# Doubling levels of a triangular inverse on every second block of columns, in a two-layer encoder kernel

## The chip, the cores and the metric

The kernel runs on one NeuronCore of a Trainium2 chip. TensorE does matrix products out of SBUF into PSUM, VectorE, ScalarE and GpSimd work elementwise, SyncE starts most transfers. The metric is the device time of one execution in microseconds, lower is better. All data are fp32. A profile records each instruction of one execution and the clock that TensorE was granted.

## What is computed

Two layers of a bidirectional encoder on 256 tokens of width 1024. Each layer has a SwiGLU block, a mixer of three branches and another SwiGLU block. The change touches the first branch, RWKV-7 time mixing with 16 heads of 64, forwards and backwards:

```python
def rwkv7_scan(r, w, k, v, a, b, reverse):
    """Generalised delta rule: S_t = S_{t-1} diag(w_t) + (S_{t-1} a_t) b_t^T + v_t k_t^T, y_t = S_t r_t."""
    ...
    def step(state, inp):
        r_t, w_t, k_t, v_t, a_t, b_t = inp
        sa = jnp.einsum("bhij,bhj->bhi", state, a_t)
        state = (state * w_t[:, :, None, :] + sa[..., None] * b_t[:, :, None, :]
                 + v_t[..., None] * k_t[:, :, None, :])
        return state, jnp.einsum("bhij,bhj->bhi", state, r_t)
```

The kernel doesn't run this token by token. It cuts the 256 tokens into 4 chunks of 64. Within a chunk the dependence of each token on the earlier ones is a triangular 64x64 matrix, and what is needed is the inverse of (identity minus that matrix), for each head, chunk and direction.

## The kernel before

**Data.** Heads are handled in pairs, 8 pairs a layer. A tile has 128 partitions: 64 for the first head of the pair, 64 for the second. The helper by_head issues one matmul for each head, 64 contraction rows and 64 weight columns each, so that the two use different quarters of the array. Each fp32 matmul appears in a trace as two weight loads and two matmul records. All matmuls have the line of the helper mm (L787), all two-tensor VectorE operations L1478 or L1484.

**One pair** (pair_body) goes in this order. First come products of the scaled keys with the stacked operands (64x192 and 64x64 forms), for each direction d, with masks on VectorE; they give the triangular matrix mb[:, d, c, 0:L] and the first inverse of 2x2 blocks, dd[:, d, 0] (called D), and its transpose dd[:, d, 1]. Pairs 1 to 3 also carry two products of the conditioning vector with 512-column weights (late_modulation), one before each half. Then comes the doubling stage, then the recurrence over the four chunks, into which the preparation of the next pair is woven (pair_lora, pair_bonus).

**The doubling stage** has LV = 5 levels. At level k the diagonal blocks of width h = 2 << k are already inverted, and the level joins two neighbours. For each direction d TensorE forms F = mb times D into PSUM bank 2 + d (8 matmuls, 64 moving columns each). VectorE multiplies F by the mask lvl[:, d, k + 1], which keeps only the blocks that join two neighbours, and writes E into ee[:, d]. TensorE forms D times E and E times the transposed D into bank 4 + d (16 matmuls for each direction; the last level forms only the second, 8). VectorE adds both onto dd[:, d] in one operation. Four semaphores hold the order: f_done, e_ready, de_done, dd_ready. TensorE's queue is F for d = 0, F for d = 1, DE for 0, DE for 1; VectorE's is mask 0, mask 1, addition 0, addition 1. VectorE waits for each of its own operations before the next one (raised). Nothing else is queued on either engine within the stage.

**Buffers.** All stage tensors are cut from one scratch tile by a carver. ee is [2, CH, L], and two buffers of the group norm, yy and ysq, lie in it. On GpSimd's queue, at the beginning of the branch, stand two loads of weights, two copies of an identity into the operand tile ar (signal eyes_ready), and then the four weight loads of pair 0 (pair_loads); everything later on that queue waits for the pairs.

Of the kernel before, what the change touches and what calls it, by code (L numbers as in the profile page):

```python
# [15 lines left out]
ALU = mybir.AluOpType  # L16
# [4 lines left out]
P = 128  # L21
# [94 lines left out]
def build(nc, a, out):  # L116
    with ExitStack() as ctx:
# [92 lines left out]
        dd = carve([2, 2, CH, L])  # L210
        ee = carve([2, CH, L])

        yy, ysq = ee[:, 0], ee[:, 1]
        rs = carve([2, L])
# [205 lines left out]
        def settle(eng):  # L420

            eng.sem_inc(settled, 1)

        block = ctx.enter_context(nc.Block())
# [109 lines left out]
        def _(pool):  # L534
# [70 lines left out]
            for l in range(DEPTH):  # L605
# [46 lines left out]
                for d in range(2):  # L652
                    ins = pool.tensor_copy(ar[:, d, :, 2, :], eye)
                    if d == 0:
                        own.step(ins)
                ins.then_inc(eyes_ready.sem, 1)
                pool.wait_ge(*eyes_ready(l, 1))
# [127 lines left out]
        def _(pe):  # L785
# [89 lines left out]
            for l in range(DEPTH):  # L875
# [104 lines left out]
                def pair_body(p, first, last, late=None):  # L980
# [29 lines left out]
                    for k in range(LV):  # L1010
                        w = p * 2 * LV + 2 * k
                        for d in range(2):
# [6 lines left out]
                            for c in range(CH):  # L1019
                                ins = by_head(ps[:, 2 + d, c * L:(c + 1) * L], mb[:, d, c, 0:L], dd[:, d, 0, c, :])  # L1020
                            ins.then_inc(f_done.sem, 1)
                        for d in range(2):
                            pe.wait_ge(*e_ready(l, w + d + 1))
                            for c in range(CH):
                                if k < LV - 1:
                                    by_head(ps[:, 4 + d, c * L:(c + 1) * L], dd[:, d, 1, c, :], ee[:, d, c, :])
                                ins = by_head(ps[:, 4 + d, S + c * L:S + (c + 1) * L], ee[:, d, c, :], dd[:, d, 1, c, :])
                            ins.then_inc(de_done.sem, 1)
# [445 lines left out]
        def _(dve):  # L1474
# [69 lines left out]
            for l in range(DEPTH):  # L1544
# [197 lines left out]
                def pair_body(p, first, last, late=None):  # L1742
# [37 lines left out]
                    for k in range(LV):  # L1780
                        w = p * 2 * LV + 2 * k
                        for d in range(2):
                            dve.wait_ge(*f_done(l, w + d + 1))
                            raised(tt(ee[:, d], ps[:, 2 + d, 0:S].rearrange("p (c t) -> p c t", c=CH),
                                      lvl[:, d, k + 1:k + 2, :].to_broadcast(b4), ALU.mult), e_ready(l, w + d + 1))
                        for d in range(2):
                            dve.wait_ge(*de_done(l, w + d + 1))
                            u0 = 0 if k < LV - 1 else 1
                            both = dd[:, d, u0:2].rearrange("p u c t -> p (u c t)")
                            raised(tt(both, both, ps[:, 4 + d, u0 * S:2 * S], ALU.add), dd_ready(l, w + d + 1))  # L1790

# [338 lines left out]
```

## Time and profile before

| | |
|---|---|
| median of 3 runs | 4291.69 us (4289.75 to 4297.94) |
| the profiled execution: its own time | 4294.79 us |
| its span, first to last instruction | 4293.1 us |
| mean granted clock of TensorE | 0.85 of full speed (1.00 is 2.4 GHz, 0.50 is 1.2 GHz) |
| busy: TensorE, weight loads, VectorE | 3354.0, 2316.1, 1398.4 us |
| the doubling stages | 16, at about 555 to 1013 us and 2690 to 3152 us |

A line of the page's groups gives line, engine, operation, the tiles written and read, their shapes, the count and the mean time. Idle time in front of a group counts only where nothing else was running that the end waits for. A busy TensorE is not one at its peak: the time of a record includes its way through the array, and records overlap; their pace shows in how many fit into a stretch.

### The profile page before, as it was taken

To read this page: it belongs to the slowest core of one execution; us is meant where nothing else is said; L and a number is where in the kernel's file an instruction comes from. 1 tells how busy PE (TensorE), PEld (TensorE's weight loads), DVE (VectorE), ACT (ScalarE), POOL (GpSimd) and SP (SyncE) were. 2 spreads that over 40 slices of the span, in tenths; PEclk is the share of its full clock that TensorE was granted. 3 is DMA by queue.
4 is the path that set the end of the run, shared out by engine and by line. 5 is a ranking of instruction groups with operands and counts; after the bars stand their busy time and mean duration, and the time that the engine had idled before them with its cause. 6 is when DMAs were issued, how large, how long until landed. Compare 5 with 4: busy or idle time off the path is not lost.

```text
span 4293.1 us, 50048 instructions
## 1 busy us (share of the span) xinstructions
PE 3354.0 (78%) x22117; PEld 2316.1 (54%) x22117; DVE 1398.4 (33%) x2502; ACT 373.8 (9%) x764; POOL 209.6 (5%) x352
## 2 busy tenths in 40 slices
PE   6998778778855588679969986887787655887798
PEld 4666565565443436447646665655554533364476
DVE  1002555662136601410010025555522266024100
ACT  0000201010111000200000011001001110001000
POOL 4000000000001100000000000000000011000000
PEclk9999888778975599789989988897898755997899
DMA  6553212001311123034445522120023120331343
GB/s 212 176 181 107 96 48 67 23 4 60 134 65 60 39 99 137 20 122 151 148 163 183 189 102 90 48 82 6 4 69 131 59 68 31 119 118 40 118 147 108
DMA packets 234938, 410.51 MB, mean 96 GB/s; under 512 B 6601, under 2 KB 101383, under 8 KB 234721
## 3 DMA queue, kind: packets, MB, share of 16 engines
q1 hardware_dynamic: 224672, 378.81, 25.6%
q0 software_dynamic: 10048, 28.49, 2.2%
q8 instruction: 174, 2.85, 0.3%
q14 instruction: 44, 0.35, 0.0%
HBM read 406.10 MB, written 1.18 MB: 95 GB/s over the span
## 4 chain that ended last, share of the span: by engine, by line
PE 65%; DVE 18%; issue 8%; DMA 4%; ACT 3%; POOL 1%; DVEq 0%; SPq 0%; POOLq 0%; ACTq 0%
PE ps L787 63%; DVE scratch L1478 7%; DVE scratch L1484 4%; DVE scratch L1481 3%; DMA ring<-in_ffn_w 1%; DMA scratch<-acs_scratch 1%; DMA ring<-in_w_in 1%; ACT scratch L1396 1%; DVE merged L1652 1%; DVE hT L1481 1%; ACT scratch L1263 0%; DMA scratch<-in_norm_w 0%; DVE scratch L1666 0%; PE ps L1132 0%; PE ps L819 0%
## 5 line engine op out<-in xcount | busy, mean ns | idle before, releaser
L787 PE MATMUL ps<-scratch 64*64 64x64 f32 (+5 forms) x14112 | 1201.7, 284 | 373.9 <-DVE scratch L1478 126.2
L787 PEld LDWEIGHTS ps<-scratch 64*64 64x64 f32 (+2 forms) x14112 | 840.0, 160 | 717.3 <-issue 203.3
L787 PE MATMUL ps<-hT,ring 128*128 128x256 f32 (+1 forms) x4992 | 1125.4, 388 | 59.6 <-DVE hT L1481 29.2
L787 PEld LDWEIGHTS ps<-hT,ring 128*128 128x128 f32 (+1 forms) x4992 | 971.0, 195 | 223.8 <-DVE hT L1481 31.4
L1478 DVE TENSOR_TENSOR scratch<-scratch,ps 128x512 f32<-128x512 f32 (+3 forms) x312 | 202.0, 647 | 1303.9 <-ACT scratch L1273 781.2
L787 PE MATMUL ps<-ring,hT 128*128 128x512 f32 x896 | 411.9, 622 | 29.9 <-DMA ring<-in_w_in 16.0
L1478 DVE TENSOR_TENSOR scratch<-scratch 128x512 f32<-128x512 f32 (+5 forms) x452 | 302.8, 670 | 61.1 <-DMA scratch<-acs_scratch 21.6
L787 PEld LDWEIGHTS ps<-ring,hT 128*128 128x128 f32 x896 | 177.9, 200 | 257.6 <-issue 223.5
L787 PE MATMUL ps<-ring,ccol 128*128 128x512 f32 x576 | 262.4, 613 | 2.4 <-DMA ring<-in_ada_w 2.4
L787 PE MATMUL ps<-ring,scratch 128*128 128x512 f32 x512 | 221.7, 592 | 0.0
L787 PEld LDWEIGHTS ps<-ring,ccol 128*128 128x128 f32 x576 | 113.4, 199 | 143.3 <-issue 137.3
L1484 DVE SCALAR_TENSOR_TENSOR scratch<-ps,prm,scratch 128x254 f32<-128x254 f32 x192 | 92.6, 482 | 234.7 <-ACTq L1399 228.3
L787 PEld LDWEIGHTS ps<-ring,scratch 128*128 128x128 f32 x512 | 97.3, 190 | 122.5 <-issue 122.5
L1132 PE MATMUL ps<-ident,scratch 128*128 128x128 f32 x80 | 19.7, 427 | 134.9 <-DVE scratch L1478 134.9
L1273 ACT ACTIVATE scratch<-ps 128x512 f32<-128x512 f32 x44 | 26.3, 597 | 1110.9 <-PE ps L787 1110.9
L1478 DVE TENSOR_TENSOR scratch<-ps,lvl 128x256 f32<-128x256 f32 x224 | 95.1, 425 | 81.9 <-PE ps L787 76.8
L1484 DVE SCALAR_TENSOR_TENSOR scratch<-ps,der,scratch 128x255 f32<-128x255 f32 (+1 forms) x112 | 54.0, 482 | 151.3 <-ACTq L1300 147.8
L1481 DVE TENSOR_SCALAR scratch<-scratch 128x64 f32<-128x64 f32 (+6 forms) x256 | 86.5, 338 | 42.8 <-ACTq L1453 19.9
L1132 PEld LDWEIGHTS ps<-ident,scratch 128*128 128x128 f32 x80 | 15.7, 223 | 139.0 <-DVE scratch L1478 139.0
L603 POOL TENSOR_TENSOR stat<-stat,mhalf 128x2 f32<-128x2 f32 x12 | 8.5, 704 | 1382.6 <-DVE stat L1481 1382.6
L819 PE MATMUL ps<-ident,scratch 128*128 128x128 f32 x96 | 21.9, 421 | 67.9 <-DVE scratch L1481 67.9
L1478 DVE TENSOR_TENSOR prow<-ps,ident 128x512 f32<-128x512 f32 x24 | 16.6, 692 | 149.4 <-PE ps L787 149.4
(206 smaller groups left out, 1339.7 us busy)
## 6 DMA issues: line engine op xcount, KB each, us to landing
ring<-in_w_in SPq DMA_DIRECT2D x56, 2048.0 KB, 7.8
ring<-in_ffn_w SPq DMA_DIRECT2D x88, 1024.0 KB, 7.9
ring<-in_ada_w SPq DMA_DIRECT2D x36, 2048.0 KB, 7.9
scratch<-in_ffn_w SPq DMA_DIRECT2D x44, 1024.0 KB, 5.1
ring<-in_w_branch_mamba SPq DMA_DIRECT2D x8, 2048.0 KB, 8.0
scratch<-acs_scratch POOLq DMA_DIRECT2D x32, 512.0 KB, 5.2
ring<-in_w_branch_rwkv SPq DMA_DIRECT2D x4, 2048.0 KB, 8.5
ring<-in_w_branch_diff SPq DMA_DIRECT2D x4, 2048.0 KB, 7.9
```

Source lines behind the costliest of these rows:

```text
L603: pool.tensor_tensor(stat[:, 4:4 + n], stat[:, 2:2 + n], mhalf[:, 0:n], ALU.pow).then_inc(rstd_ready.sem, 1)
L787: return pe.matmul(o, lhsT, rhs, start=start, stop=stop)
L819: ins = pe.transpose(o, xn[:, t, kt * P:(kt + 1) * P], ident[:, :])
L1132: ins = pe.transpose(ps[:, 4 + t, m * P:(m + 1) * P], cv[:, parity, m, t * P:(t + 1) * P], ident[:, :])
L1273: act.activation(sgm[:, j % 2, :], ps[:, 2 * (g % 2), :], ACT.Sigmoid).then_inc(ffn_sig.sem, 1)
L1396: own.step(act.activation(cv[:, parity, m, :], ps[:, 2 * ((g + parity) % 2) + m // 2, (m % 2) * S:(m % 2 + 1) * S], ACT.Identity, scale=pr ...
L1478: return dve.tensor_tensor(o, i0, i1, op)
L1481: return dve.tensor_scalar(o, i0, s1, s2, op0, op1)
L1484: return dve.scalar_tensor_tensor(out=o, in0=i0, scalar=s, in1=i1, op0=op0, op1=op1)
L1652: own.step(dve.reciprocal(kk_sq_buf, kk_sq_buf))
```

## The change

At each level only every second block of the columns can change: for direction 0 the even blocks of D and the odd ones of its transpose, for direction 1 the other way round. The new kernel computes, masks and adds these columns alone. The moving operand of each matmul of the stage is a view of every second block (32 columns in runs of h), its result is packed in PSUM (32 columns for each chunk). The mask reads and writes only the half blocks, and the addition reads 128 packed columns for each of the two products and adds them onto the half blocks of dd. E remains a full 64-column weight operand, whose other blocks have to be zero. So ee becomes five buffers, one for each level, cleared once per layer by GpSimd, and yy and ysq get a space of their own. The numbers of matmuls, weight loads, VectorE operations and semaphore steps stay; one memset per layer is added.

```diff
--- before.py
+++ after.py
@@ -208,9 +208,9 @@
         mb = carve([2, CH, 2 * L])
         mk = carve([2, CH, 2 * L])
         dd = carve([2, 2, CH, L])
-        ee = carve([2, CH, L])
-
-        yy, ysq = ee[:, 0], ee[:, 1]
+        ee = carve([LV, 2, CH, L])
+        yy = carve([CH, L])
+        ysq = carve([CH, L])
         rs = carve([2, L])
         yn = carve([CH, L])
         gstat = carve([4, CH])
@@ -421,6 +421,31 @@
 
             eng.sem_inc(settled, 1)
 
+        def half_blocks(m, k, side):
+
+            return m.rearrange("p (b u i) -> p b u i", u=2, i=2 << k)[:, :, side, :]
+
+        def half_chunks(m, k, side):
+
+            return m.rearrange("p c (b u i) -> p c b u i", u=2, i=2 << k)[:, :, :, side, :]
+
+        def joined(m, k):
+
+            return m.rearrange("p (b i) -> p b i", i=2 << k)
+
+        def half_pair(d, k, us):
+
+            h = 2 << k
+            flat = dd.rearrange("p d u c t -> p (d u c t)")
+            at = d * 2 * S
+            if us == 1:
+                m = flat[:, at + S + (1 - d) * h:at + S + (1 - d) * h + S - h].rearrange("p (a n i) -> p a n i", a=1, i=h)
+            elif d == 0:
+                m = flat[:, at:at + 2 * (S + h)].rearrange("p (a n i) -> p a n i", a=2, i=h)
+            else:
+                m = flat[:, at + h:at + h + 2 * (S - h)].rearrange("p (a n i) -> p a n i", a=2, i=h)
+            return m[:, :, 0:2 * (S // (2 * h)) - 1:2, :]
+
         block = ctx.enter_context(nc.Block())
 
         def halves(pair):
@@ -653,7 +678,8 @@
                     ins = pool.tensor_copy(ar[:, d, :, 2, :], eye)
                     if d == 0:
                         own.step(ins)
-                ins.then_inc(eyes_ready.sem, 1)
+                own.step(ins)
+                pool.memset(ee, 0.0).then_inc(eyes_ready.sem, 1)
                 pool.wait_ge(*eyes_ready(l, 1))
                 own.restart()
                 def pair_loads(q):
@@ -1017,14 +1043,17 @@
                             else:
                                 pe.wait_ge(*btm_evac(l, 2 * p + 2))
                             for c in range(CH):
-                                ins = by_head(ps[:, 2 + d, c * L:(c + 1) * L], mb[:, d, c, 0:L], dd[:, d, 0, c, :])
+                                ins = by_head(joined(ps[:, 2 + d, c * 32:(c + 1) * 32], k), mb[:, d, c, 0:L],
+                                              half_blocks(dd[:, d, 0, c, :], k, d))
                             ins.then_inc(f_done.sem, 1)
                         for d in range(2):
                             pe.wait_ge(*e_ready(l, w + d + 1))
                             for c in range(CH):
                                 if k < LV - 1:
-                                    by_head(ps[:, 4 + d, c * L:(c + 1) * L], dd[:, d, 1, c, :], ee[:, d, c, :])
-                                ins = by_head(ps[:, 4 + d, S + c * L:S + (c + 1) * L], ee[:, d, c, :], dd[:, d, 1, c, :])
+                                    by_head(joined(ps[:, 4 + d, c * 32:(c + 1) * 32], k), dd[:, d, 1, c, :],
+                                            half_blocks(ee[:, k, d, c, :], k, d))
+                                ins = by_head(joined(ps[:, 4 + d, P + c * 32:P + (c + 1) * 32], k), ee[:, k, d, c, :],
+                                              half_blocks(dd[:, d, 1, c, :], k, 1 - d))
                             ins.then_inc(de_done.sem, 1)
                     pe.wait_ge(*dd_ready(l, (p + 1) * 2 * LV))
 
@@ -1781,13 +1810,16 @@
                         w = p * 2 * LV + 2 * k
                         for d in range(2):
                             dve.wait_ge(*f_done(l, w + d + 1))
-                            raised(tt(ee[:, d], ps[:, 2 + d, 0:S].rearrange("p (c t) -> p c t", c=CH),
-                                      lvl[:, d, k + 1:k + 2, :].to_broadcast(b4), ALU.mult), e_ready(l, w + d + 1))
+                            h = 2 << k
+                            found = ps[:, 2 + d, 0:P].rearrange("p (c b i) -> p c b i", c=CH, i=h)
+                            keep = half_chunks(lvl[:, d, k + 1:k + 2, :], k, d).to_broadcast([P, CH, L // (2 * h), h])
+                            raised(tt(half_chunks(ee[:, k, d], k, d), found, keep, ALU.mult), e_ready(l, w + d + 1))
                         for d in range(2):
                             dve.wait_ge(*de_done(l, w + d + 1))
                             u0 = 0 if k < LV - 1 else 1
-                            both = dd[:, d, u0:2].rearrange("p u c t -> p (u c t)")
-                            raised(tt(both, both, ps[:, 4 + d, u0 * S:2 * S], ALU.add), dd_ready(l, w + d + 1))
+                            both = half_pair(d, k, 2 - u0)
+                            gain = ps[:, 4 + d, u0 * P:2 * P].rearrange("p (u n i) -> p u n i", u=2 - u0, i=2 << k)
+                            raised(tt(both, both, gain, ALU.add), dd_ready(l, w + d + 1))
 
                     for j in range(CH):
                         dve.wait_ge(*r_done(l, 4 * p + j + 1))
```

## Rows read from the trace of the kernel before

**Rows 1.** The page: busy time by engine, granted clock by slice, the chain's engines.
```profile
PE 3354.0 (78%) x22117; PEld 2316.1 (54%) x22117; DVE 1398.4 (33%) x2502; ACT 373.8 (9%) x764; POOL 209.6 (5%) x352
...
PEclk9999888778975599789989988897898755997899
...
PE 65%; DVE 18%; issue 8%; DMA 4%; ACT 3%; POOL 1%; DVEq 0%; SPq 0%; POOLq 0%; ACTq 0%
```
**Rows 2.** VectorE's groups by form: names, shapes, count | busy us, mean ns, idle before.
```profile
L1478 DVE TENSOR_TENSOR scratch<-scratch,ps 128x512 f32<-128x512 f32 x232 | 159.7, 688 | 889.3 <-ACT scratch L1273 781.2 <-PE ps L787 105.8
...
L1478 DVE TENSOR_TENSOR scratch<-ps,lvl 128x256 f32<-128x256 f32 x224 | 95.1, 425 | 81.9 <-PE ps L787 76.8
...
L1794 DVE COPY scratch<-ps 128x128 f32<-128x128 f32 x64 | 18.7, 292 | 59.3 <-PE ps L787 59.3
```
**Rows 3.** The chain of waits, pair 2 of layer 0: start us, us, what.
```profile
688.29 0.70 DVE scratch L1478
...
689.03 2.57 PE ps L787 x80
...
691.70 0.70 DVE scratch L1478
...
699.48 0.70 PE ps L787 x16
...
700.27 0.44 DVE scratch L1478
...
700.75 0.70 PE ps L787 x16
...
701.55 0.43 DVE scratch L1478
```
**Rows 4.** Windows, 64 columns on 128: busy of PE, PEld, DVE, ACT, POOL (count), clock, DMA.
```profile
3621.30:3634.80 13.50, 13.50 (x64) 13.50 (x64) 7.21 (x9) 0.00 (x0) 0.00 (x0) 0.50 0.00 0
1298.90:1302.30 3.40, 3.40 (x33) 3.40 (x31) 0.71 (x2) 2.26 (x4) 0.00 (x0) 1.00 0.56 177
```
**Rows 5.** Timeline of TensorE, 64 columns on 64: start us, us, what [idle before].
```profile
588.02 0.69 PE L787 MATMUL ps<-scratch 64*64 64x64 f32 x8 [0.46 <-DVE scratch L1801]
...
713.01 2.44 PE L787 MATMUL ps<-scratch 64*64 64x64 f32 x40 [0.23 <-DVE scratch L1794]
```
**Rows 6.** Windows of six stretches: as in rows 4.
```profile
555.60:570.00 14.40, 13.39 (x410) 12.59 (x412) 9.29 (x17) 0.00 (x0) 0.00 (x0) 1.00 0.01 3
588.10:593.40 5.30, 5.30 (x30) 3.43 (x31) 4.70 (x12) 0.00 (x0) 1.04 (x1) 0.51 0.00 0
593.60:599.00 5.40, 5.40 (x15) 2.23 (x15) 1.84 (x3) 0.00 (x0) 0.00 (x0) 1.00 0.00 0
683.80:686.00 2.20, 1.14 (x33) 1.00 (x32) 1.93 (x4) 0.00 (x0) 0.00 (x0) 1.00 0.41 66
713.00:715.40 2.40, 2.38 (x40) 2.25 (x40) 1.82 (x5) 1.34 (x3) 0.00 (x0) 0.50 0.04 10
789.60:794.60 5.00, 5.00 (x42) 3.88 (x44) 0.34 (x1) 0.00 (x0) 0.00 (x0) 0.50 0.00 0
```
**Rows 7.** The chain of waits, three doubling stages: pauses of TensorE.
```profile
626.47 0.88 issue
...
2767.07 0.71 issue
...
2894.72 0.97 issue
```
**Rows 8.** Timeline of GpSimd at the beginning of the branch, layer 0.
```profile
388.66 0.87 POOL L653 COPY scratch<-stack_i 128x256 f32<-128x256 f32 x2
...
390.25 0.59 POOL L662 DMA_DIRECT2D scratch<-in_rwkv_w  x1 [0.71 <-POOL scratch L653]
...
522.27 0.57 POOL L662 DMA_DIRECT2D scratch<-in_rwkv_w  x1 [129.85 <-PE ps L787]
```
**Rows 9.** The instructions on one tile: GpSimd's largest memset, min/median/max ns.
```profile
L596 POOL MEMSET vfirst<- x1: 1805/1805/1805, 96.5 to 96.5; 128x2048 f32 x1
```

## Prediction

> **What bounds the kernel now.** I read the page first: TensorE is busy 78% of the span and carries 65% of the chain that ended last, VectorE 18% [rows 1]. The granted clock is not uniform: several slices stand at 5 to 8 tenths [rows 1]. Then I read the forms by line to get prices, then the chain of waits inside one doubling stage. There are 16 such stages (8 head pairs, 2 layers), all alike in form. In one steady level the chain is: the second addition of the level before (0.70 us), 0.04 us until TensorE starts, 80 matmul records (2.57 us), 0.10 us until VectorE starts the next addition (691.70 - 689.03 - 2.57) [rows 3]. A record is half a matmul: each fp32 matmul shows as two. The period is 691.70 to 688.29 = 3.41 us. TensorE has 96 records per level; 16 of them (the first half of F) run under the addition, the other 80 (second half of F, 32 of DE for each direction) stand on the path, and the masks lie beside them. The last level has no D half and is a ladder: 16 records 0.70, mask 0.44, 16 records 0.70, addition 0.43 [rows 3]. No DMA, ScalarE or GpSimd step stands in this stage. What ends a level is therefore the pace of the records plus one addition.
>
> **The masks.** 128x256 becomes 128x128. Prices: 425 ns now; 292 ns for 128x128 out of PSUM (a copy, the nearest row) [rows 2]. 133 ns less. On the path this counts only for the mask of the first level (it waits for F and DE waits for it) and for the second mask of the last level: 2 x 0.13 = 0.26 us per stage.
>
> **The additions.** In levels 0 to 3, 128x512 becomes 128x256: 688 to 425 ns (the price of the 128x256 masks, one PSUM and one SBUF operand as well) [rows 2], four on the path: 4 x 0.26 = 1.05 us. In the last level 128x256 becomes 128x128: 0.13 us. The first half of F then starts earlier too, but still ends before the second half may start. The new patterns have runs of 2, 4, 8, 16 and 32 floats, and no VectorE row shows a run shorter than 64. Bounds: no extra cost, or each element of the two shortest runs costs double, which puts masks and additions of those two levels back at the old prices (0.13 + 2 x 0.26 = 0.66 us per stage back). I take no extra cost, since runs of 64 with gaps (the initial masks, in the same group of 224) cost the same 425 ns as dense ones [rows 2]. Below nothing it can't go: the element count is what falls.
>
> **The matmuls.** The moving columns fall from 64 to 32; the number of matmuls, of weight loads and the 64 weight columns stay. Does the pace follow? The trace has a case with few moving columns for its weights: 64 moving columns on 128 weight columns. At full clock 31 weight loads take 3.40 us, 110 ns each, and at the lower clock 64 take 13.50 us, 211 ns [rows 4]; there are eight such stretches, all at 0.50, of which the last is shown. With the same 64 moving columns on 64 weight columns, two heads side by side, one record follows another every (2.57 - 0.70)/64 = 29.2 ns at full clock [rows 3], 58 ns per head, and every (2.44 - 0.69)/32 = 54.7 ns at the lower clock [rows 5, 6]. The same moving columns, half the weight columns, half the time: in these cases the pace follows the weights. So the change leaves 29.2 ns per record. Only the tail of the last record of each block gets shorter; its size isn't shown, I take 0.03 us (6 blocks on the path: about 0.16 us), bounds 0 and 0.05. The other bound for the pace is half of 29.2 ns (rival 2).
>
> The Trainium skill (TensorE: Matmul & The Clock Gate, Back-to-back issue gap) has another floor to the same effect: matmuls of 1 to 64 columns all take about 60 cycles. By that sentence as well the sum keeps its matmul term.
>
> **Sum with the clock as it was:** 0.26 + 1.05 + 0.13 + 0.16 = 1.6 us per stage, 16 stages, 25.6 us. Against the profiled execution (4294.8 us; span 4293.1) that is 4269.2, and 3.1 less for the median of the runs shown (4291.7): 4266.
>
> **The clock.** The stages now run at 1.00 (2.4 GHz) once entered: 555.6 to 570 us at 1.00 [rows 6]. What the engine does before the clock rises or stays is what the change alters. Two stretches in which the records call TensorE busy without a gap go different ways: from 588.1 to 593.4 (64 on 64 columns, then 128 on 256 and 512) the clock is 0.51 and then 1.00 [rows 6]; in all eight stretches of 64 moving on 128 weight columns, 13.5 us each, it stays at 0.50 to the end [rows 4]. There the array streams columns only half of the time that weights are loaded. After the change, the doubling stage has just that ratio: 32 moving on 64 weight columns. So I expect: a stage that is at the lower clock can't climb out of it before its last level is over; and a stage entered at the full clock is much nearer to losing it at every gap than now. The gaps are there: between F and DE of the first level in pairs 1 and 2 VectorE reduces a row first (TensorE busy 1.14 of 2.20 us) [rows 6], and three stages of 16 hold a pause of 0.71 to 0.97 us that the chain calls issue [rows 7]. Today these gaps go by at full clock.
>
> Price of a fall: at 54.7 ns a level is 96 x 54.7 = 5.25 us (TensorE alone, the additions hidden under F) against 3.41, +1.84 per level; in the ladder 32 + 16 records more slowly and two smaller VectorE steps, about +0.6 against now; the start of the recurrence behind it, some 80 records at +25 ns until the clock is back, +2.0. A fall at the pause in the second level costs 2.5 x 1.84 + 0.6 + 2.0 = 7.2 us, one in the first level 4 x 1.84 + 0.6 + 2.0 + 0.8 (rest of its DE) = 10.8 us.
>
> I take five stages: the three with a pause (7.2 each = 21.6), and two more of those with the long gap after F or entered just as the clock rises (10.8 each = 21.6). Eleven stages gain 1.6 = 17.6. Net +25.6: 4294.8 + 25.6 - 3.1 = **4317 us**. What no row says is how near to falling a steady level is. A second unknown: in pairs 4 to 7 the products ahead of each stage start at 0.50 [rows 6], and a rise that doesn't come earlier when they do would eat up to 8 x 1.6 = 13 us of the gain.
>
> **The buffers.** One factor buffer per level instead of one: DE reads all 64 weight columns of it, so the half that isn't written must be zero. GpSimd clears 128x2560 per layer: its 128x2048 clear took 1.81 us [rows 9], so 2.26 us, behind the two copies at 388.66 and ahead of the four loads of pair 0, the first of which starts at 390.25. Those loads then start 2.3 us later; the next command of that queue waits until 522.27 for TensorE [rows 8], so the cover is 130 us. Behind it in GpSimd's queue are only these loads; who waits for them is the first pair's projection, long after. Cost nothing; 2 x 2.3 us without the cover. The moved group-norm buffers add no wait, as VectorE writes them in order.
>
> A rule that speaks against the change would be one on short strides. The Trainium skill (Advanced Engine Details and Errata, Memory Cachelines) asks for at least two hits in a 16-byte line; two floats of every four give exactly two. By it no read slows; if the matmul's read did slow at runs of 2, there is room: its columns now take about half of each record's slot. No row here shows such a read.
>
> **Rivals.**
> 1. The full clock holds, or falls in a stage or two only. For it: today even the pauses pass at 1.00, the steady level keeps 96 records in a shorter period. Against: the eight stretches. Time 4266 with none, up to 4280 with one or two. Chance 0.21. It is on the other side (faster).
> 2. The pace follows the moving columns after all: 80 records at 14.6 instead of 29.2 ns take 1.2 us less per level, some 5 us per stage; 4266 - 80 = 4186. Against it rows 4. Chance 0.04.
> 3. The two cancel: two or three stages fall (some 20 to 30 us back against 21 to 24 gained), or the gain of pairs 4 to 7 is lost ahead of the next stage: 4283 to 4300. Chance 0.15. Short runs that cost VectorE double belong here: 16 x 0.66 = 10.6 us back, 4277, and with one fall 4287.
> 4. A steady level too is beyond what holds the full clock: 13 or more of the 16 fall in their first level: 13 x 10.8 - 3 x 1.6 = +136, 4428. Chance 0.10. It decides from the first level on; the sign is that of the forecast.
> The forecast (3 to 8 stages fall, net gain of time lost 10 to 70 us): 0.50.
>
> **How the numbers follow.** The likeliest case gives 4317; its own range is 4301 to 4362. The range reaches down to 4264 for rival 1 and up to 4352, leaving out rival 2, rival 4 and the top of the forecast case, about 2 in 10. About 0.2% (8.6 us) is what a measurement of this kernel can tell from no change. Faster: 0.21 + 0.04 = 0.25. Same: 0.15. Slower: 0.50 + 0.10 = 0.60.
>
> **What would show it.** VectorE masks at 292 and additions at 425 ns show the first terms; a record pace of 29 ns with 32 columns the third; a steady level of 3.1 us at clock 1.00 the sum. Level stages with a granted clock of 0.50 and levels of 5.2 us show the fall, with the stages of 626 us and 2767 us first. I am wrong if all 16 stages stand at 1.00, if the records come closer than 29 ns, or if steady levels fall without a gap.

## The result, and the profile after

Four runs of the changed kernel have a median of 4349.9 us (4339.3 to 4353.5), four of the kernel before beside them 4293.0 us (4289.8 to 4297.9). The ratio is 1.0127, interval 1.0107 to 1.0148: slower by 57 us at the medians. The profiled execution took 4339.3 us, its span is 44.4 us longer than before. The forecast was slower by 26.

Two words are used throughout: a matmul or a stage is narrow when its records move 32 columns and wide when they move 64; a stage holds when its granted clock stays at 1.00 and falls when it drops to 0.50 (1.2 GHz) within it.

The page of the kernel after: span; busy time by engine; granted clock of TensorE in 40 slices; the chain's engines. They answer to [rows 1].

```profile
span 4337.5 us, 50050 instructions
...
PE 3424.2 (79%) x22117; PEld 2401.4 (55%) x22117; DVE 1338.5 (31%) x2502; ACT 373.6 (9%) x764; POOL 214.0 (5%) x354
...
PEclk9999777777985589699989987787779755897899
...
PE 67%; DVE 16%; issue 8%; DMA 4%; ACT 3%; POOL 1%; DVEq 0%; SPq 0%; POOLq 0%; ACTq 0%
```

VectorE has 60 us less work, as meant. TensorE is busy 70 us longer with the same number of matmuls, and slices 6 to 10 (where the doubling stages of layer 0 lie) read 77777 where they read 88778, and slices 26 to 30 (layer 1) read 78777 where they read 89789. VectorE's forms, line 1507 (the helper for two tensors), the same columns as [rows 2]:

```profile
L1507 DVE TENSOR_TENSOR scratch<-scratch,ps 128x256 f32<-128x256 f32 x128 | 54.0, 422 | 120.9 <-PE ps L813 120.9
...
L1507 DVE TENSOR_TENSOR scratch<-ps,lvl 128x128 f32<-128x128 f32 x160 | 46.7, 292 | 54.0 <-PE ps L813 52.0
```

Masks take 292 ns and the additions of the first four levels 422 ns in the mean over runs of 2 to 32 floats, no more than the prices of dense rows (292 and 425 ns): here short runs cost nothing on VectorE. The chain of waits in pair 6 of layer 0, a stage that keeps the full clock (start us, us, what), answers to [rows 3]:

```profile
943.69 2.54 PE ps L813 x80
...
946.33 0.43 DVE scratch L1507
...
946.80 2.55 PE ps L813 x80
...
949.44 0.43 DVE scratch L1507
...
958.04 0.30 DVE scratch L1507
```

The period is 949.44 - 946.33 = 3.11 us where it was 3.41. The 80 records still take 2.55 us: halving the columns left the pace alone. In this stage the change does what it was costed at. Now the stages by windows: 14.5 us from the first mask of twelve of the 16 (the eight of layer 0, then pairs 1, 2, 3 and 7 of layer 1). Columns: window, length, busy of PE, PEld, DVE, ACT, POOL (count), clock, DMA.

```profile
552.40:566.90 14.50, 13.73 (x432) 13.06 (x432) 6.71 (x20) 0.00 (x0) 0.00 (x0) 1.00 0.02 5
616.20:630.70 14.50, 14.13 (x278) 14.13 (x280) 4.28 (x12) 0.00 (x0) 0.00 (x0) 0.54 0.38 143
689.30:703.80 14.50, 14.04 (x300) 13.93 (x300) 4.81 (x14) 0.00 (x0) 0.00 (x0) 0.61 0.38 141
759.00:773.50 14.50, 13.63 (x424) 12.84 (x420) 6.71 (x20) 0.00 (x0) 0.00 (x0) 1.00 0.44 149
813.90:828.40 14.50, 14.50 (x298) 14.45 (x296) 4.48 (x13) 0.00 (x0) 0.00 (x0) 0.55 0.01 2
878.90:893.40 14.50, 14.50 (x295) 14.45 (x294) 4.38 (x13) 0.00 (x0) 0.00 (x0) 0.55 0.01 2
943.80:958.30 14.50, 13.61 (x431) 12.90 (x428) 6.84 (x20) 0.00 (x0) 0.00 (x0) 1.00 0.02 5
1001.70:1016.20 14.50, 14.50 (x296) 14.50 (x298) 4.38 (x13) 0.00 (x0) 0.00 (x0) 0.55 0.01 2
2780.20:2794.70 14.50, 14.11 (x278) 14.11 (x280) 4.29 (x13) 0.00 (x0) 0.00 (x0) 0.54 0.39 142
2852.70:2867.20 14.50, 13.44 (x374) 13.00 (x376) 5.67 (x16) 0.00 (x0) 0.00 (x0) 0.87 0.38 143
2919.90:2934.40 14.50, 12.77 (x316) 12.29 (x314) 4.86 (x14) 0.00 (x0) 0.00 (x0) 0.79 0.44 149
3155.50:3170.00 14.50, 14.50 (x296) 14.45 (x294) 4.38 (x13) 0.00 (x0) 0.00 (x0) 0.55 0.01 2
```

Read the count beside the clock. A stage at 1.00 gets through all 432 records in 14.5 us; one at 0.55 gets through some 296 and is not done for another 8 us, while TensorE shows busy without a gap. Nine stages lose the clock: pairs 1, 2, 4, 5, 7 of layer 0, and pairs 1, 2, 3, 7 of layer 1. Before, all 16 stood at 1.00. The fall within pair 4, and the stretches behind a stage that held (pair 6) and one that fell (pair 4):

```profile
813.90:815.30 1.40, 1.40 (x52) 1.35 (x48) 0.58 (x2) 0.00 (x0) 0.00 (x0) 1.00 0.00 0
815.30:818.00 2.70, 2.70 (x60) 2.70 (x56) 0.88 (x3) 0.00 (x0) 0.00 (x0) 0.52 0.02 6
818.00:828.00 10.00, 10.00 (x192) 10.00 (x192) 2.82 (x8) 0.00 (x0) 0.00 (x0) 0.50 0.01 2
...
958.30:962.30 4.00, 3.92 (x80) 3.92 (x80) 1.18 (x5) 0.00 (x0) 0.00 (x0) 0.57 0.01 4
958.30:1001.70 43.40, 29.82 (x386) 23.64 (x386) 24.04 (x54) 5.79 (x14) 1.01 (x1) 0.65 0.01 1
836.10:878.90 42.80, 28.68 (x390) 22.55 (x392) 24.08 (x54) 5.79 (x14) 3.20 (x5) 0.68 0.03 6
```

The clock falls 1.4 us into the stage and stays at its lower level (1.2 GHz) until the stage is over. And the stage that held loses it just behind its end: the first 4 us of the recurrence behind pair 6 run at 0.57. The same stretches in the kernel before:

```profile
939.30:943.30 4.00, 4.00 (x89) 3.31 (x89) 1.15 (x4) 0.00 (x0) 0.00 (x0) 1.00 0.01 4
939.30:981.20 41.90, 28.36 (x384) 22.00 (x386) 24.02 (x54) 5.79 (x14) 1.01 (x1) 0.67 0.00 1
```

The 43.4 us from the end of a held stage to the next were 41.9. With the stage itself that is 57.9 us, where it was 58.1 (16.2 + 41.9): the 1.6 us that a held stage gains are not kept here.

**The sums.** From the first mask to the last addition of each stage, the 16 stages took 262.4 us before and 296.4 after (+34.0). The 14 stretches between two stages of a layer took 621.3 and 636.8 (+15.6). The rest (start, between the layers, end) is 5.2 less, for which I have no reason. Together +44.4, the difference of the spans. Stage by stage there is one trace, and it is of the fastest of the four runs; its mean clock is 0.825, that of the others 0.822 to 0.824.

### The profile page after: what moved, and what is told of

The parts are those of the page before. It is cut to its first block, busy times and chain, and to the rows that moved or that the text cites. A ratio compares the mean times of both kernels' runs of the same rounds, so it can differ in the third digit from the quotient of the medians.

```text
span 4337.5 us, 50050 instructions
## 1 busy us (share of the span) xinstructions
PE 3424.2 (79%) x22117; PEld 2401.4 (55%) x22117; DVE 1338.5 (31%) x2502; ACT 373.6 (9%) x764; POOL 214.0 (5%) x354
## 4 chain that ended last, share of the span: by engine, by line
PE 67%; DVE 16%; issue 8%; DMA 4%; ACT 3%; POOL 1%; DVEq 0%; SPq 0%; POOLq 0%; ACTq 0%
PE ps L813 65%; DVE scratch L1507 6%; DVE scratch L1513 4%; DVE scratch L1510 3%; DMA ring<-in_ffn_w 1%; DMA scratch<-acs_scratch 1%; DMA ring<-in_w_in 1%; ACT scratch L1425 1%; DVE merged L1681 1%; DVE hT L1510 1%; ACT scratch L1292 0%; DVE scratch L1695 0%; PE ps L1161 0%; DMA scratch<-in_norm_w 0%; PE ps L845 0%
## 5 line engine op out<-in xcount | busy, mean ns | idle before, releaser
L813 PE MATMUL ps<-scratch 64*64 64x32 f32 (+6 forms) x14112 | 1278.0, 306 | 350.9 <-DVE scratch L1507 105.8
L813 PEld LDWEIGHTS ps<-scratch 64*64 64x64 f32 (+2 forms) x14112 | 928.4, 185 | 681.4 <-issue 204.6
L1507 DVE TENSOR_TENSOR scratch<-scratch,ps 128x256 f32<-128x256 f32 (+3 forms) x312 | 163.5, 524 | 1376.0 <-ACT scratch L1302 780.3
L813 PE MATMUL ps<-ring,hT 128*128 128x512 f32 x896 | 410.7, 620 | 30.1 <-DMA ring<-in_w_in 16.2
L1507 DVE TENSOR_TENSOR scratch<-ps,lvl 128x128 f32<-128x128 f32 (+1 forms) x224 | 73.9, 330 | 102.6 <-PE ps L813 99.1
L1510 DVE TENSOR_SCALAR scratch<-scratch 128x64 f32<-128x64 f32 (+6 forms) x256 | 86.3, 337 | 42.8 <-ACTq L1482 19.9
```

What stands on the lines that cost most here:

```text
L813: return pe.matmul(o, lhsT, rhs, start=start, stop=stop)
L1507: return dve.tensor_tensor(o, i0, i1, op)
L1510: return dve.tensor_scalar(o, i0, s1, s2, op0, op1)
```

## The experiments

The theory (A): it is the records with 32 moving columns on 64 weight columns that bring the clock down, and a stage made of them is near its edge. The rivals: the longer chain or the buffers; only the entry or the pauses; the gapped reads. This table has all runs; "fell" counts stages with a clock under 1.00 in the profiled execution, the last two columns are the sums just explained. The median of the kernel before lies between 4290.7 and 4296.7 us in the sets that the variants ran beside, so that the ratios compare better than the medians.

| kernel | median us | ratio to before | fell | 16 stages | 14 between |
|---|---|---|---|---|---|
| before | 4293.0 | 1 | 0 | 262.4 | 621.3 |
| after | 4349.9 | 1.0127 (1.0107 to 1.0148) | 9 | 296.4 | 636.8 |
| wide_pe | 4262.7 | 0.9926 (0.9909 to 0.9942) | 0 | 240.8 | 616.1 |
| de_wide | 4264.3 | 0.9931 (0.9916 to 0.9946) | 1 | 242.4 | 614.3 |
| f_wide | 4270.7 | 0.9945 (0.9928 to 0.9962) | 3 | 249.3 | 617.7 |
| buffers_only | 4297.2 | 1.0009 (1.0000 to 1.0018) | 0 | 261.9 | 621.6 |
| first_level_wide | 4303.1 | 1.0033 (1.0020 to 1.0046) | 4 | 255.1 | 638.9 |
| last_level_wide | 4312.6 | 1.0035 (1.0019 to 1.0050) | 10 | 306.3 | 620.2 |
| ends_wide | 4278.0 | 0.9961 (0.9946 to 0.9976) | 5 | 258.7 | 615.0 |
| slow_add_narrow | 4407.0 | 1.0270 (1.0255 to 1.0285) | 16 | 360.9 | 637.0 |
| slow_add_wide | 4292.1 | 1.0002 (0.9993 to 1.0012) | 0 | 264.4 | 619.8 |
| dense_reads | 4352.2 | 1.0135 (1.0114 to 1.0156) | 10 | 301.0 | 642.8 |
| late_spread_narrow | 4339.9 | 1.0109 (1.0094 to 1.0124) | 10 | 293.9 | 635.9 |
| late_spread_wide | 4255.5 | 0.9917 (0.9902 to 0.9931) | 0 | 243.3 | 606.8 |

**All matmuls wide again (wide_pe).** TensorE computes all 64 columns into full blocks; VectorE still masks and adds only its half, in place.

```diff
-ins = by_head(joined(ps[:, 2 + d, c * 32:(c + 1) * 32], k), mb[:, d, c, 0:L],
-              half_blocks(dd[:, d, 0, c, :], k, d))
+ins = by_head(ps[:, 2 + d, c * L:(c + 1) * L], mb[:, d, c, 0:L], dd[:, d, 0, c, :])
```

> The matmuls of the doubling stage are back to 64 moving columns (F, and both products of DE), written unpacked as before; VectorE's masks and additions stay on half the columns and read them out of PSUM in place. Nothing of the result is left out. Theory A (the clock falls because the matmuls stream half as many columns for the same weight loads): all 16 doubling stages at a granted clock of 1.00, a steady level of 3.12 to 3.15 us, a stage near 14.6 us against 16.15 before; time 4263 to 4275. Theory B (the clock falls because of VectorE's side: shorter steps, strided patterns, or the new buffers): 6 or more stages fall to 0.50 again, 4325 to 4355.

Measured 4262.7 us. Two of its stages (pairs 4 and 6 of layer 0) and the stretch behind pair 6:

```profile
802.90:817.40 14.50, 13.77 (x430) 12.87 (x426) 6.69 (x20) 0.00 (x0) 0.00 (x0) 1.00 0.01 3
...
912.20:926.70 14.50, 13.73 (x430) 12.83 (x425) 6.69 (x20) 0.00 (x0) 0.00 (x0) 1.00 0.02 5
...
926.90:930.90 4.00, 4.00 (x89) 3.31 (x89) 1.15 (x4) 0.00 (x0) 0.00 (x0) 1.00 0.01 4
926.90:966.70 39.80, 24.92 (x386) 19.52 (x388) 24.00 (x54) 5.79 (x14) 1.01 (x1) 0.83 0.01 1
```

The same number of matmuls and weight loads as after, the same VectorE sizes. What differs is the moving columns per record, and with them two patterns: TensorE reads without gaps (dense_reads tries that alone), and its results lie in PSUM unpacked (that alone was not tried). No stage falls, and 87 us are gone. The narrow columns themselves gave 0.16 us a stage (14.68 us here, 14.52 in a held stage after); the other 1.47 us are VectorE's half-size steps.

**One kind of matmul wide (de_wide, f_wide).** de_wide: D and E with 64 columns (64 of the 96 records of a level), F with 32. f_wide the other way.

```diff
-by_head(joined(ps[:, 4 + d, c * 32:(c + 1) * 32], k), dd[:, d, 1, c, :], half_blocks(ee[:, k, d, c, :], k, d))
+by_head(ps[:, 4 + d, c * L:(c + 1) * L], dd[:, d, 1, c, :], ee[:, k, d, c, :])
```

> The changed kernel with DE alone (64 of a level's 96 records) back to 64 moving columns; F stays at 32, VectorE at half. Nothing is left out. Theory A: no stage or one falls, 4263 to 4280, at or below the kernel with wide F. Theory B: 7 to 10 fall, 4325 to 4355.

> The changed kernel with F alone (32 of a level's 96 matmul records) back to 64 moving columns; DE stays at 32, VectorE at half. Nothing is left out. Theory A: fewer stages fall than the 9 of the changed kernel, 1 to 4 of 16, first those with a pause of TensorE or the long gap in the first level; 4270 to 4305. Theory B (not the matmul columns): as many as before, 7 to 10, 4325 to 4355.

With two thirds of the records wide one stage falls (pair 3 of layer 1, after a pause of TensorE of 1.2 us), and only for 3.4 us:

```profile
2878.20:2881.60 3.40, 3.40 (x72) 3.40 (x70) 0.71 (x2) 0.00 (x0) 0.00 (x0) 0.51 0.02 5
2881.60:2887.50 5.90, 5.29 (x160) 4.82 (x156) 3.00 (x9) 0.00 (x0) 0.00 (x0) 1.00 0.01 3
```

With one third wide, three fall, each about 8 us into the stage, in the third level, behind a pause (pair 1 of both layers, pair 3 of layer 1). With 0, 32, 64 and 96 narrow records in a level 0, 1, 3 and 9 stages fall, and neither kind alone gives the nine; whether the share or the kind decides between 1 and 3 isn't told apart.

**The buffers alone (buffers_only).** The kernel before, with a factor buffer for each level, GpSimd's clear and the moved group-norm buffers.

```diff
-ee = carve([2, CH, L])
+ee = carve([LV, 2, CH, L])
+pool.memset(ee, 0.0).then_inc(eyes_ready.sem, 1)
```

> The kernel before with only the buffers of the change: one factor buffer for each level, cleared by GpSimd, and own buffers for the group norm. All operations keep 64 columns. Theory A: 4288 to 4298, stages at 1.00 and 16.15 us, the clear of about 2.3 us under the projection. Rival (the moved buffers or the clear in GpSimd's queue cost): 4300 or more, with the first stage later.

Ratio 1.0009, interval 1.0000 to 1.0018, so that a cost of up to 8 us isn't excluded by the times; the stages (261.9 us) and stretches (621.6 us) are as before, and nothing of the 57 us lies in them. The clear in the kernel after, in GpSimd's timeline:

```profile
386.59 2.23 POOL L682 MEMSET scratch<- 128x2560 f32 x1
...
389.53 0.59 POOL L688 DMA_DIRECT2D scratch<-in_rwkv_w  x1 [0.71 <-remote]
```

It takes 2.23 us (the step said 2.26).

**Only the first level wide, only the last, both.** Levels two to four stay narrow in all three.

```diff
-ins = by_head(joined(...), mb[:, d, c, 0:L], half_blocks(...))
+if k in WIDE:                      # {0}, {4}, {0, 4}
+    ins = by_head(ps[:, 2 + d, c * L:(c + 1) * L], mb[:, d, c, 0:L], dd[:, d, 0, c, :])
+else:
+    ins = by_head(joined(...), mb[:, d, c, 0:L], half_blocks(...))
```

> The changed kernel, but the first of the five doubling levels computes all 64 columns again (matmuls into full blocks, VectorE still masks and adds only its half, in place); levels two to five stay at 32 columns. Theory A (a level whose records carry 32 columns on 64 weight columns gives the clock too little to go by wherever it stands, so that entry decides only part of it): the first level no longer loses the clock, some stages fall later, in levels two or three, at a lower price each (about 4 us instead of 6 to 8); 4285 to 4320 us, with 4 to 9 of 16 stages showing a level at 0.50. Rival B (only the entry decides: the lower half rate of the products ahead, the gap between F and DE of the first level, and the first level itself): once the first level is wide, no stage falls but perhaps the three with a pause, and the time is that of the all-wide variant within a few us, 4260 to 4272.

> Only the last of the five levels computes all 64 columns, levels one to four stay at 32. Theory A: the falls inside the stages stay as in the changed kernel (7 to 10 of 16, in the first or second level); what goes is the late start of the recurrence behind the stages that hold, up to 3.5 us each for about seven stages: 4320 to 4340. Rival C: as the changed kernel, 4345 to 4355.

> First and last of the five levels compute all 64 columns, levels two to four stay at 32. In the traces so far, a narrow stage that held the full clock loses it behind its last level, whose matmuls alternate with VectorE steps: the first 4 us of the recurrence stand at 0.57, and the stretch from stage to stage is 43.4 us, against 39.9 behind a wide stage. Theory A (each narrow stretch brings the clock down behind it, the last level as well): with a wide last level the stretches behind pairs 4 to 7 are 39.8 to 40.1 us, 8 x 3.5 = 28 us less than the first_level_wide variant's 4303: 4270 to 4283, while the falls in levels three and four of the stages with a pause stay (3 to 5 stages). Rival C (the stretch behind the stage depends on when in the recurrence the clock changes, not on the last level): 43 us stays, 4298 to 4306.

first_level_wide: 4303.1 us, inside theory A's numbers, but for half another reason. Four stages fall (pairs 1 and 2 of layer 0, 1 and 3 of layer 1, all in the third or fourth level). Not one of pairs 4 to 7 falls, which rival B had said; where there is neither pause nor long gap, the first level decides in this trace. Of its 36 us over wide_pe in the spans, 14 lie in the stages and 23 in the stretches between. ends_wide tells what these are: behind the same pair 6, first first_level_wide, then ends_wide:

```profile
939.30:943.30 4.00, 4.00 (x80) 3.96 (x80) 1.15 (x4) 0.00 (x0) 0.00 (x0) 0.57 0.02 4
939.30:982.70 43.40, 29.93 (x386) 23.73 (x388) 23.98 (x53) 5.78 (x14) 1.01 (x1) 0.65 0.01 1
```

```profile
934.50:938.50 4.00, 3.93 (x88) 3.27 (x88) 1.16 (x5) 0.00 (x0) 0.00 (x0) 1.00 0.02 4
934.50:974.40 39.90, 24.95 (x386) 19.53 (x388) 24.03 (x55) 5.79 (x14) 1.01 (x1) 0.83 0.01 1
```

With the last level wide the recurrence starts at 1.00 and the stretch is 3.5 us shorter; all 14 together 638.9 - 615.0 = 24 us, of which the six behind pairs 4 to 6 have 20.5. The medians give 25 us (31 by the ratios, as the two ran beside other sets). So a narrow last level, whose 16-record blocks alternate with VectorE steps, costs a clock drop behind the stages of pairs 4 to 7 that hold; behind pairs 0 and 3, where other work follows, a held narrow stage shows none. Rival C's numbers fall, but not all of its idea. The width of the last level is not the whole reason: slow_add_wide (below) has it wide and starts the recurrence behind pair 6 at 1.00, yet its stretch is 41.6 us:

```profile
939.40:943.40 4.00, 3.95 (x88) 3.27 (x88) 1.15 (x4) 0.00 (x0) 0.00 (x0) 1.00 0.02 4
939.40:981.00 41.60, 27.56 (x386) 21.22 (x388) 23.98 (x53) 5.78 (x14) 1.01 (x1) 0.71 0.00 1
```

Stage and stretch together are 57.9 us there, 58.1 before and 57.9 after, but 54.5 in wide_pe and ends_wide. By the clock records the last rise ahead of the next stage comes 55.9 us behind the first mask of pair 6 in the first three and 52.4 us behind it in the last two: in these five what a stage saves counts only where that rise comes earlier too. last_level_wide repairs only what lies behind the stage: the stretches go from 636.8 to 620.2, the falls stay (10). Its median, 4312.6, is lower than theory A had said; its runs spread from 4302 to 4329 us, and the profiled one is the slowest of them, with a mean clock of 0.832 against 0.837 to 0.839 in the others, so how many stages fall probably differs from run to run. Only one execution has a trace, so that this isn't shown.

**A hole in each level (slow_add_narrow, slow_add_wide).** One more VectorE copy, 128x128, ahead of each second addition, on the kernel after and on wide_pe.

```diff
 dve.wait_ge(*de_done(l, w + d + 1))
+if d == 1:
+    own.step(dve.tensor_copy(yn[:, 0:2, :].rearrange("p c t -> p (c t)"), ps[:, 4, 0:P]))
```

> The changed kernel with one VectorE copy of 128x128 out of PSUM (about 0.3 us) ahead of the second addition of each level: TensorE gets a hole of about 0.34 us in each of the levels at full clock, and the VectorE chain is about as long as before the change. Theory A (what the full clock wants is columns streamed over time; narrow records are near the limit, so a small hole in each level tips it): nearly all 16 stages fall in the first or second level; at the lower clock the copy is hidden (a level of 5.12 us is TensorE alone), so the stage takes about 22.5 us; 16 x (22.5 - 14.6) = +126 on the 4267 of no falls and a few us for the gaps behind: 4385 to 4415. Rival B (the falls come from particular places, the gaps at the entry and pauses; the steady level is safe): as many falls as in the changed kernel (9 of 16), and the copies add 7 stages x 5 x 0.3 = 10 us: 4350 to 4365.

> The same copy ahead of the second addition, on the variant whose matmuls carry all 64 columns. Theory A: no stage falls; the hole is paid at full clock, 16 x 5 x 0.31 = 25 us on the 4262.7 of the all-wide variant: 4280 to 4292, clock 0.85 or 0.86. If holes of TensorE as such lost the clock, whatever the columns, stages would fall here too and the time would be above 4340.

Pair 6 of layer 0, first narrow (first 3.7 us, then the rest of the stage), then wide (the whole stage):

```profile
967.70:971.40 3.70, 3.25 (x108) 3.08 (x106) 1.96 (x6) 0.00 (x0) 0.00 (x0) 1.00 0.02 4
971.40:989.60 18.20, 17.26 (x328) 16.71 (x325) 6.30 (x19) 0.00 (x0) 0.00 (x0) 0.53 0.01 3
```

```profile
923.10:939.40 16.30, 13.77 (x431) 12.87 (x426) 8.31 (x25) 0.00 (x0) 0.00 (x0) 1.00 0.01 4
```

The same hole: narrow, all 16 stages fall, +57 us over after; wide, none falls and the copies cost 4292.1 - 4262.7 = 29 us, their plain length (80 levels x 0.32 = 26). That is the strongest evidence for theory A: a hole of this size loses no clock where the records are wide, and all 16 stages where they are narrow. A miss in it: at the lower clock the copy was to be hidden, but a level takes 5.39 us instead of 5.12.

**Reads without gaps (dense_reads).** The 32 moving columns are the first 32 of the block; the inverse computed is another one.

```diff
-return m.rearrange("p (b u i) -> p b u i", u=2, i=2 << k)[:, :, side, :]
+return m[:, 0:32].rearrange("p (b i) -> p b i", i=2 << k)
```

> The changed kernel with one edit on TensorE: the 32 moving columns of every doubling matmul are the first 32 of their block, without gaps, instead of every second run of 2, 4, 8, 16 or 32. The inverse it computes is therefore another one (the output isn't the reference's); number and size of all instructions stay. Theory A (what brings the clock down is that each record carries 32 columns, not how they are read): records at 29 ns at full clock, 7 to 11 stages fall, 4338 to 4360. Rival D (the gapped reads of TensorE cost something that lowers the clock or slows the rise): few or no stages fall, the stretches behind pairs 4 to 7 are near 40 us, 4262 to 4275.

Ratio 1.0135, ten stages fall; the interval holds the ratio of the change. The pattern of TensorE's reads is not the cause. Of pairs 4 to 7 of layer 0, pair 5 held here and pair 6 fell; after it was the other way:

```profile
881.90:896.40 14.50, 13.58 (x430) 12.86 (x426) 6.84 (x20) 0.00 (x0) 0.00 (x0) 1.00 0.01 3
939.80:954.30 14.50, 14.50 (x298) 14.45 (x294) 4.42 (x13) 0.00 (x0) 0.00 (x0) 0.55 0.02 3
```

The work of these stages is the same, so which of them fall is not a property of the pair. The traces show what goes with it: where the clock's last rise ahead of the stage lies. The 2.1 us up to the first mask of pairs 4 to 7 of layer 0, kernel after:

```profile
811.82:813.92 2.10, 1.34 (x30) 0.99 (x28) 1.40 (x3) 1.23 (x5) 0.00 (x0) 0.96 0.00 0
876.79:878.89 2.10, 1.34 (x32) 0.96 (x30) 1.55 (x3) 1.24 (x5) 0.00 (x0) 0.99 0.00 0
941.71:943.81 2.10, 1.34 (x32) 0.96 (x30) 1.58 (x3) 1.24 (x5) 0.00 (x0) 1.00 0.00 0
999.59:1001.69 2.10, 1.34 (x28) 0.82 (x24) 1.89 (x3) 1.24 (x5) 0.00 (x0) 0.97 0.00 0
```

Pair 6 (the third line) held; its clock had risen 2.13 us before the first mask, that of the three that fell 1.95 to 2.08 us before it. Four traces have a narrow first level and no added copy (after, last_level_wide, late_spread_narrow, dense_reads). In their 32 stages of pairs 4 to 7 the 15 that held had that rise 2.11 to 2.54 us before the first mask; of the 17 that fell, 15 had it 1.95 to 2.09 us before, and two 2.12 and 2.19. So it is less a matter of chance than of some tenths of a microsecond at the entry. No run moved this on purpose; it stays a correlation.

**The late steps moved (late_spread_narrow, late_spread_wide).** VectorE's modulation steps of pairs 1 to 3 (0.69, 0.69 and 0.16 us), which stood between F and DE of the first level, go behind the masks of levels two to four.

```diff
-if late:
-    late_modulation(p, 1, 7)
+held = late_steps(p, 1, 7) if late else []
 for k in range(LV):
...
+        if held and k:
+            held.pop(0)()
```

> The changed kernel (32 columns everywhere) with VectorE's late modulation steps moved from ahead of the first level to behind the masks of levels two to four, so that the long gap between F and DE of the first level is gone in pairs 1 and 2. Theory A: a hole at the entry is one of the things that tip a narrow stage; pairs 1 and 2 of both layers (four of the nine that fell) fall later or only at their pause in level two or three, while pairs 4, 5 and 7 stay as they are: about 4 x 2 to 7 us of falls and 4 us of moved steps less: 4310 to 4340. Rival B': the gap does nothing to the clock (these stages fall as before, in the first level) and only the moved steps come off: 4342 to 4352.

> The all-wide variant with the late modulation steps of VectorE (0.69 us product with the identity, 0.69 us reduction, 0.16 us addition, which stand between the two m2 masks and the first doubling level in pairs 1 and 2; one addition in pair 3) moved behind the masks of levels two, three and four, where VectorE waits for DE. No stage falls in either theory; the move takes about 1.1 to 1.5 us off each of four stages and about 0.5 off two: 4 to 7 us less than the 4262.7 of the all-wide variant, 4255 to 4260. If the steps are not hidden there (the slot is about 0.64 us of VectorE, then 0.42 of addition and 0.5 of slot), each costs back what it took and the time stays 4262.

Narrow: 4339.9 us, at the edge of both expectations, and the interval overlaps that of after. The trace shows more: pair 1 of both layers no longer falls in its first level (1.2 us in) but 9.1 us in, behind the pause, which fits a gap that tips them; but the last rise ahead of these stages also lies elsewhere now (8.0 us before the first mask, it was 9.0), and the two aren't told apart. It helped little, as the pauses remained and again four of the eight stages of pairs 4 to 7 fell. Wide: 4255.5 us, the fastest of all, with 9.3 us less between the stages (616.1 to 606.8) and 2.5 more in them. Against before it is 0.8% faster. Against wide_pe the intervals of the ratios overlap; that it beats that one is argued from the stretches, not shown by the times.

## Why the prediction was right or wrong

**Direction and mechanism: right.** Slower, by falls of the clock in the doubling stages, with levels of 5.12 us (5.25 said) at 0.50 that in this kernel don't climb out before the end.

**The small terms: right.** Masks 292 ns; additions 422 to 425; levels of 3.11 us; a held stage 14.52 instead of 16.15 us, 1.63 (1.6 said). The record pace with 32 columns stays: the block of 80 takes 2.55 us where it took 2.57, so it is still 29 ns each. Rival 2 is dead. The Trainium skill (TensorE: Matmul & The Clock Gate, "Wait — 56ns, not 53.3ns?") puts the floor between small matmuls at about 25 ns; the trace agrees in kind, and 29 ns is what counts here.

**The step that failed: "I take five stages"**, and with it "a steady level" that needs a gap or a pause. It was nine. Pairs 4, 5 and 7 of layer 0 and pair 7 of layer 1 fell with neither, 1.4 us after their first mask. In pairs 4 to 7 four of eight fell after, four in last_level_wide, four in late_spread_narrow and five in dense_reads; none of eight in first_level_wide and ends_wide. So in these pairs the narrow first level is where a stage is lost, in 17 of 32. Those that come through it at full clock keep it. In pairs 1 to 3 most later falls follow a pause, but not all: pair 2 of layer 0 falls 3.2 us in (after) and pair 3 of layer 0 9.0 us in (last_level_wide) with no idle time of TensorE above 0.2 us ahead of it. I had drawn the sign "if steady levels fall without a gap" as what would prove me wrong, and it did.

**The price of a fall was too high, which hid part of that.** 10.8 us were said for one in the first level. Measured, pair 4: 22.2 us against 16.15 (+6.1), and the stretch behind 42.8 against 41.9 (+0.9): 7.0. The 3.8 too much are (levels counted from first mask to first mask): the fall comes 1.4 us into the level, so that it takes 4.04 us and not 5.25, and the 0.8 for "rest of its DE" isn't there (2.0 together); levels 0.13 shorter each (0.4); the ladder +0.3 and not +0.6; behind it 0.9 and not 2.0 (1.1). A fall at a pause was priced 7.2; the three in pairs 2 and 3 that came later than the first level cost 1.3 (pair 2 of layer 1), 3.3 (pair 3 of layer 1) and 5.0 us (pair 2 of layer 0) in the stage. The two errors offset each other, which was luck: nine falls at the prices of the forecast (six of 10.8, three of 7.2, seven stages gaining 1.6) would have been +75, five at the measured 5.0 and eleven gains of 1.6 would have been +7 in the stages.

**The unknown that was named came in where stages held.** "A rise that doesn't come earlier when they do would eat up to 8 x 1.6 = 13 us": behind pair 6 of layer 0 a held stage gives back 43.4 - 41.9 = 1.5 of its 1.6, and the last rise ahead of the next stage stands where it stood, 55.9 us behind the first mask. The sum had left this out. It isn't a fixed price: with wide matmuls and VectorE's halves (wide_pe) the rise comes at 52.4 and the stretch is 39.8, and the last level has most of the part in it (ends_wide).

**The sum made anew, on the spans.** Seven held stages: 113.4 to 102.5 us, -10.9 (forecast for eleven: -17.6). Nine fallen: 149.0 to 193.9, +44.9, or 5.0 each (forecast for five: 43.2, with what lies behind). Stretches +15.6. Rest -5.2. Together +44.4. The median of the four runs lies another 10.6 us above the profiled run.

**The buffers, and the pause stages.** No cost of the buffers is told from zero (ratio 1.0009). All three falls of f_wide and the one of de_wide come behind a pause: the pauses were a part of the cause, not its bound. The part of the long gap fits late_spread_narrow and isn't shown apart.

**Rival 1's number was not a floor.** The time without any fall was put at 4266; wide_pe has 4262.7. That they are near is in part luck: the 25.6 us were to come from the stages alone, and wide_pe gains 21.6 in them, 5.2 between them and 1.5 elsewhere.

## What to carry to other kernels

Before cutting the moving columns of small fp32 matmuls, see whether the record pace follows them; where it is set by the weights, the cut saves next to no time on TensorE (0.16 us of a stage of 14.7 here) and can cost it the full clock, as it did in nine stages of 16. Cut the work of the engine that ends the wait (here VectorE) and leave TensorE's columns wide: the same idea, half done, is 0.7% faster than before, and done in full 1.3% slower. Price a loss of the clock by where it happens and what comes behind, and try it with a small hole made on purpose: the narrow kernel fell in all 16 stages, the wide one in none.

## What was not expected of the hardware

- TensorE can be busy without a gap and stay at the lower clock (192 records in 10.00 us at 0.50), while wide records with 5% of idle time stay at 1.00 (13.77 of 14.50 us). The Trainium skill (TensorE: Matmul & The Clock Gate, Part 1: The HAM clock gate) ties the gate to how busy the engine has been; by these rows the busy time of the trace doesn't tell which stages keep the clock.
- The same instructions go either way: of eight like stages four fell, and which ones goes with some tenths of a microsecond between the clock's last rise and the stage. One narrow variant spreads more from run to run (4302 to 4329 us in last_level_wide) than the kernel before (4289 to 4299 us beside it); others (late_spread_narrow, 4339 to 4349) don't.
- A wide last level goes with another clock in the 40 us behind it (ends_wide 0.83 in the mean, first_level_wide 0.65), though the matmuls there are untouched. Why the clock is higher late in that stretch too was not tried; the kernel before, with a wide last level as well, stands at 0.67 there.
- What the clock follows stays open. Shown is that it falls with narrow records and not with wide ones (wide_pe against after, slow_add_wide against slow_add_narrow), with the same number of matmuls, weight loads and VectorE steps; the packing of the results in PSUM changed with the width and wasn't tried alone.
